# Rests of weights between the table passes, small loads on GpSimd's queue, two output products at attention's end, and TensorE's first expert pass written out

## The chip, the cores and the metric

The kernel runs on 1 core of one Trainium2 chip. The metric is the device time of one launch in microseconds (us): 1806.31 us, the median of 3 runs from 1805.55 to 1809.32. The profiled execution, from which all rows here come, took 1809.38 us, of which the profile covers a span of 1807.4 us from the first to the last instruction.

## The reference, cut to what matters

Two layers over 256 tokens of width 1024. Each layer projects the normalised input once, runs three mixers on columns of that projection, and adds a channel mixer: dense in layer 0, 8 experts of which each token uses 2 in layer 1.

```python
for i in range(DEPTH):                       # 2 layers
    h = rmsnorm(x, norm_mix[i])
    z = h @ w_in[i]                          # [S5 512 | q, k, v 3 x 768 | memory q 512 | gates 3 x 1024]
    y_ssm = ssm_branch(z[..., :c0], ...) @ w_ssm_out[i]   # scan over time, GELU, GLU with w_glu (512 x 1024)
    y_att = dilated_attention(...) @ w_att_out[i]         # QK-norm, rotary with positions
    mem_n = rmsnorm(mem, norm_mem[i])
    y_mem = memory_attention(z[..., c3:c4], mem_n, w_mem_kv[i], ...) @ w_mem_out[i]
    g = sigmoid(z[..., c4:]).reshape(bsz, L, 3, D)
    merged = g[..., 0, :] * y_ssm + g[..., 1, :] * y_att + g[..., 2, :] * y_mem
    x = x + merged @ w_o[i]
    h2 = rmsnorm(x, norm_ffn[i])
    x = x + (swiglu(h2, ...) if i == 0 else moe_swiglu(h2, ...))   # 8 experts, 1024 x 3584
```

## The kernel before, in words

All five engines run programs written out by hand, joined by semaphores. What follows is what the change touches.

**Weights.** A layer's mixer takes its weights in tiles of 128x2048 fp32 (1 MB), numbered in the order of use: 0 to 3 are `w_mem_kv`, 4 to 25 halves of twelve-column-block `w_in`, 26 and 27 `w_glu`, 28 to 30 the last of `w_in` (30 is `IN_FULL`, 256 columns), 31 and 32 `w_ssm_out`, 33 `w_att_out`, 34 and 35 `w_mem_out`, 36 to 39 `w_o`. SP loads a tile into one of three slots of `ring` when TensorE is done with the tile three before. Products are made of two parts: ScalarE's `weights_high` copies the tile to `hi_m` (rounded, two halves of 1024 columns, L1313), and VectorE's `weights_low` subtracts that from the tile to give `ring_lo`, the rest (two halves, L1831). `hi_m` has two buffers, and so ScalarE's copy of tile m waits until TensorE is done with tile m-2:

```python
act.wait_ge(full[n % R], 16 * (n // R + 1))
if i >= 2:
    act.wait_ge(*mixer_use(l, i - 2))
```

TensorE then makes 24 groups of matmuls of each tile: high by high (L694), high by rest (L695) and rest by high (L696). The copy, the rest and the product of one tile stand each at a fixed place of their engine's program, so the order of the three programs decides who waits.

**The start of layer 0.** TensorE does tiles 0 and 1, transposes of `x` (L687), tiles 2 to 6, and then, in the S5 part, tile 7 onward. VectorE does in this order: `setup` (memory's operands and rests of tiles 0 and 1), `constants` (masks' integer grids), `state_rates`, `rotary_angles` (L1898 to L1819), rest of tile 2, `state_coefficients`, rest 3, `input_low` (L1843, the rests of x's transposes), rest 4, `state_matrices` (L1950 on), rest 5, `table_turns`, rest 6, `table_coarse` (L1973, 16 operations), `table_fine` (L1981, 16), `table_folds` (L1988, L1989). The three table functions make the angles for the rotation that turns the complex recurrence into a real scan; ScalarE takes their sines and cosines in two pieces (`tables`, L1354 and L1355).

**The S5 part.** `ssm` starts with rest 7 and then has four rounds v = 0 to 3. A round multiplies TensorE's input part by the tables (L2025, L2026), makes the rest of one tile, adds, scans (L2039), makes another rest and turns the states back (L2045, L2046); GpSimd forms the states from that (L660, L661), and TensorE's `state_output` (L875) waits for GpSimd. On TensorE the four state outputs stand behind the tiles 9, 11, 13 and 15, called here the first to the fourth state output. So round 0 makes rests 8 and 9, round 1 rests 10 and 11, round 2 rests 12 and 13, round 3 rests 14 and 15, and rest 16 follows the rounds. In both orders the first of a round's two rests stands ahead of the scans, the second behind them.

**Small loads.** SP issues, behind tile 2's load and ahead of tile 3's, the six S5 matrices of layer 0 (`load_matrices`, L420 and L423, 128 KB each) and four rows of gains for q and k (L459). GpSimd issues the same six for layer 1 later.

**Attention's end.** Attention runs in 14 slots. In a slot TensorE transposes probabilities (`pr`, L930), multiplies them with the values (L947) and fills in one tile of the list `FILL`. Slot 11 fills in only the transposes of the scan's output (L979), slot 12 tile 30, slot 13 tile 31. After the slots come 12 transposes for the other branches (L687), then tile 32, then tile 33. ScalarE's `soT_hi` (L1546) and VectorE's `soT_lo` are the two parts of the transposed scan output, the operand of tiles 31 and 32.

**Experts.** TensorE's program for the experts (`one_pass`) is a loop of three rounds with two experts each, and the last two experts after it; inside an expert there are shorter loops. ScalarE's is written out, VectorE's has a loop too. The second call of `one_pass` runs only when an expert is over 128 tokens.

Of the kernel before, what the change touches and what calls it, by code (L numbers as in the profile page):

```python
# [16 lines left out]
ALU = mybir.AluOpType  # L17
# [15 lines left out]
def decoder_trunk(nc, x_in, mem_in, positions, norm_mix, w_in, a_re, a_im, log_dt, b_re, b_im,  # L33
# [57 lines left out]
    with ctx:  # L91
# [83 lines left out]
        eb("hole", [P, BANK])  # L175
# [14 lines left out]
        invf = sb1("invf", [P, HD // 2])  # L190
        dist_i = sb1("dist_i", [P, C, SEQ], I32)
        grid_i = sb1("grid_i", [P, 2, SEQ], I32)
        ang = sb1("ang", [P, C, HD // 2])
        turns = sb1("turns", [P, C, HD // 2])
# [233 lines left out]
        def _(sp):  # L428
# [117 lines left out]
        def _(pool):  # L546
# [23 lines left out]
            def second_matrices(l):  # L570
# [27 lines left out]
                nc.gpsimd.memset(mT[:], 0.0).then_inc(sem("mT_zero"), 1)  # L598
                if l == 0:
# [39 lines left out]
            for l in range(L):  # L639
                rsqrt_mean(rs[:, 2:2 + C], ss[:, 2:2 + C], D, (sem("x_squared"), 2 * l + 1), sem("x_rs"))  # L640
                if l == 0:
                    pool.wait_ge(sem("grid_ready"), 1)
                    for c in range(C):
                        for g in range(NG):
                            last = nc.gpsimd.affine_select(out=gmask(c, g), in_=gmask(c, g), compare_op=ALU.is_ge, fill=NEG,
                                                           base=c * P, pattern=[[-1, (c + 1) * P]], channel_multiplier=1)
                    last.then_inc(sem("mask_ready"), 1)
                    second_matrices(0)
                    pool.wait_ge(sem("rope_ready"), 1)
                    pool.wait_ge(params, 16 * 2 * L)  # L650
                    rotary_gains(0)
# [1879 lines left out]
```

## Time and profile before

| | us |
|---|---|
| median of 3 runs | 1806.31 |
| runs | 1805.55, 1806.31, 1809.32 |
| the profiled execution's own time | 1809.38 |
| its span | 1807.4 |
| TensorE busy | 1765.5 (98% of the span) |
| VectorE busy | 1442.2 (80%) |
| ScalarE busy | 1175.7 (65%) |
| GpSimd busy | 112.9 (6%) |
| mean granted TensorE clock | 0.99 of full |

The profiled execution is 3.07 us over the median, so a sum that is made against it is moved by that much to stand on the median. Shares of busy time are means over the whole kernel: the change touches the first 150 us, two stretches of 30 us at 250 and 730 us, and the edges of the expert rounds at 1071, 1318 and 1565 us.

### The profile page before, as it was taken

What the parts mean: (1) busy time and instruction counts of PE and PEld (TensorE: products, weight loads), DVE (VectorE), ACT (ScalarE), POOL (GpSimd) and SP (SyncE); (2) the same over time, 40 slices, a digit from 0 to 9 for tenths busy, and PEclk for the clock granted to TensorE, in tenths of its full rate; (3) what the DMA queues carried; (4) which work ended last, traced back from release to release, by engine and by line L of the source; (5) the groups of instructions that cost most, each with busy time, mean ns of one, the idle gap of its engine ahead of it and who ended that gap; (6) DMA issues with size and microseconds to landing.
All of it is one profiled execution on the core that took longest, in us unless ns stands there. A gap on an engine that the chain in (4) does not pass through costs nothing.

```text
span 1807.4 us, 23380 instructions
## 1 busy us (share of the span) xinstructions
PE 1765.5 (98%) x8755; PEld 1461.0 (81%) x8755; DVE 1442.2 (80%) x1336; ACT 1175.7 (65%) x1320; POOL 112.9 (6%) x159
## 2 busy tenths in 40 slices
PE   7799999999999999999999999999999999999998
PEld 5688888888888888887888878888878888888886
DVE  7987547667756955568899888898888988988987
ACT  6567555654456665656776767777767767777775
POOL 3331000122001300000000000000000000000000
PEclk9899999999999999999999999999999999999999
DMA  6344435755544443377999999999999999999994
GB/s 208 117 141 140 140 99 179 229 188 185 186 139 146 151 145 119 119 267 287 373 364 335 372 348 356 376 341 362 366 330 375 364 334 372 356 364 378 351 374 183
DMA packets 227630, 477.17 MB, mean 264 GB/s; under 512 B 16012, under 2 KB 40712, under 8 KB 227528
## 3 DMA queue, kind: packets, MB, share of 16 engines
q1 hardware_dynamic: 227144, 474.99, 74.0%
q8 instruction: 67, 1.10, 0.2%
q0 software_dynamic: 288, 0.79, 0.2%
q14 instruction: 35, 0.29, 0.0%
q10 hardware_dynamic: 96, 0.02, 0.0%
HBM read 474.71 MB, written 1.05 MB: 263 GB/s over the span
## 4 chain that ended last, share of the span: by engine, by line
PE 91%; DVE 4%; ACT 2%; issue 1%; SPq 1%; DMA 1%; DVEq 0%; ACTq 0%
PE ps L694 28%; PE ps L696 27%; PE ps L695 27%; PE ps L1179 1%; PE ps L947 1%; DVE lo L2231 1%; PE ps L919 1%; PE ps L687 1%; PE ps L1157 1%; PE ps L875 1%; DVE ring_lo L1831 1%; PE ps L930 1%; DMA ring<-in_w_mem_kv 1%; SPq L420 0%; DVE sintab L1981 0%
## 5 line engine op out<-in xcount | busy, mean ns | idle before, releaser
L2231 DVE TENSOR_TENSOR lo<-ring_e,hi 128x2048 fp32r<-128x2048 f32 x288 | 657.7, 2289 | 86.9 <-ACT hi L1598 84.7
L1598 ACT ACTIVATE hi<-ring_e 128x2048 fp32r<-128x2048 f32 x288 | 552.1, 1917 | 168.5 <-PE ps L696 168.0
L694 PE MATMUL ps<-hi,xe_hi 128*128 128x512 f32 x896 | 356.0, 397 | 4.8 <-issue 4.8
L696 PE MATMUL ps<-hi,xe_lo 128*128 128x512 f32 x896 | 350.0, 391 | 0.0
L695 PE MATMUL ps<-lo,xe_hi 128*128 128x512 f32 x896 | 349.9, 390 | 0.0
L1313 ACT ACTIVATE hi_m<-ring 128x1024 fp32r<-128x1024 f32 x160 | 160.7, 1055 | 152.8 <-PE ps L696 150.3
L1831 DVE TENSOR_TENSOR ring_lo<-ring,hi_m 128x1024 fp32r<-128x1024 f32 x160 | 190.6, 1233 | 35.1 <-ACT hi_m L1313 34.6
L696 PE MATMUL ps<-hi_m,xT_lo 128*128 128x512 f32 (+1 forms) x528 | 204.7, 388 | 0.0
L694 PEld LDWEIGHTS ps<-hi,xe_hi 128*128 128x128 f32 x896 | 168.5, 188 | 41.7 <-issue 6.6
L696 PEld LDWEIGHTS ps<-hi,xe_lo 128*128 128x128 f32 x896 | 168.7, 188 | 36.5
L695 PEld LDWEIGHTS ps<-lo,xe_hi 128*128 128x128 f32 x896 | 168.9, 189 | 33.2
L694 PE MATMUL ps<-hi,aT_hi 128*128 128x512 f32 x464 | 181.6, 391 | 0.0
L696 PE MATMUL ps<-hi,aT_lo 128*128 128x512 f32 x464 | 180.8, 390 | 0.0
L695 PE MATMUL ps<-lo,aT_hi 128*128 128x512 f32 x464 | 180.6, 389 | 0.0
L694 PE MATMUL ps<-hi_m,in_hi 128*128 128x512 f32 (+1 forms) x416 | 166.6, 401 | 9.8 <-DVE ring_lo L1831 9.5
L695 PE MATMUL ps<-ring_lo,in_hi 128*128 128x512 f32 (+1 forms) x416 | 159.8, 384 | 0.0
L2231 DVE TENSOR_TENSOR lo<-hT,hi 128x2048 fp32r<-128x2048 f32 x48 | 109.9, 2289 | 14.8 <-ACT hi L1598 14.4
L696 PEld LDWEIGHTS ps<-hi_m,xT_lo 128*128 128x128 f32 x528 | 100.0, 189 | 22.0
L1598 ACT ACTIVATE hi<-hT 128x2048 fp32r<-128x2048 f32 x48 | 92.0, 1916 | 20.8 <-PE ps L696 20.8
L694 PEld LDWEIGHTS ps<-hi_m,in_hi 128*128 128x128 f32 x416 | 79.7, 192 | 29.6 <-DVE ring_lo L1831 9.7
L696 PEld LDWEIGHTS ps<-hi,aT_lo 128*128 128x128 f32 x464 | 87.1, 188 | 18.4
L694 PEld LDWEIGHTS ps<-hi,aT_hi 128*128 128x128 f32 x464 | 87.1, 188 | 18.2 <-issue 0.4
(397 smaller groups left out, 2502.2 us busy)
## 6 DMA issues: line engine op xcount, KB each, us to landing
ring_e<-in_moe_w_gate SPq DMA_DIRECT2D x104, 1024.0 KB, 6.0
ring_e<-in_moe_w_up SPq DMA_DIRECT2D x96, 1024.0 KB, 6.3
ring_e<-in_moe_w_down SPq DMA_DIRECT2D x88, 1024.0 KB, 5.7
ring<-in_w_in SPq DMA_DIRECT2D x50, 1024.0 KB, 5.1
hT<-in_moe_w_down SPq DMA_DIRECT2D x24, 1024.0 KB, 5.8
hT<-in_moe_w_up SPq DMA_DIRECT2D x16, 1024.0 KB, 5.5
ring<-in_ffn_w_gate SPq DMA_DIRECT2D x22, 512.0 KB, 4.0
ring<-in_ffn_w_up SPq DMA_DIRECT2D x22, 512.0 KB, 5.0
```

The costliest lines, as they stand in the source:

```text
L687: last = nc.tensor.transpose(o, a, ident[0:a.shape[0], 0:a.shape[0]])
L694: nc.tensor.matmul(o, x_hi, w_hi, start=first, stop=False, skip_group_check=True)
L695: nc.tensor.matmul(o, x_hi, w_lo, start=False, stop=False, skip_group_check=True)
L696: return nc.tensor.matmul(o, x_lo, w_hi, start=False, stop=end, skip_group_check=True)
L875: last = nc.tensor.matmul(y, by[:, j, r, :], wv[v % 2][:, 2 * i + h, r, :], start=False, stop=r == 1, skip_group_check=True)
L919: last = nc.tensor.matmul(ps[:, bank, col:col + nk], qkT[o:o + HD, 0, hd // 2, c * P:(c + 1) * P], qkT[o:o + HD, 1, hd // 2, 0:nk], start= ...
L930: nc.tensor.transpose(ps[:, 6 + b // 4, b % 4 * P:(b % 4 + 1) * P], pr[:, u % 2, b * P:(b + 1) * P], ident[:])
L947: last = nc.tensor.matmul(ps[:, 5, o:o + v.shape[1]], pT[:, b * P:(b + 1) * P], v, start=first, stop=end, skip_group_check=True)
L1313: nc.scalar.activation(hi_m[:, m % 2, o], ring[:, n % R, o], ACT.Copy).then_inc(sem("mixer_hi_ready"), 1)
L1598: nc.scalar.activation(hi[:, m % H, :], src, ACT.Copy).then_inc(sem("hi_ready"), 1)
L1831: V.tensor_tensor(ring_lo[:, n % R, o], ring[:, n % R, o], hi_m[:, m % 2, o].bitcast(F32), ALU.subtract).then_inc(sem("mixer_lo_ready"), 1)
L2231: last = V.tensor_tensor(lo[:, m % H, :], src, hi[:, m % H, :].bitcast(F32), ALU.subtract)
```

## The change

In layer 0, the rests of tiles 7 and 8 are made between the table passes; each round of the S5 part then makes the rests of tiles one further on (9 and 10, 11 and 12, 13 and 14, 15 and 16), and none follows the rounds. Layer 1 keeps the old order there. `rotary_angles` moves from ahead of rest 2 to behind rest 6 (its buffers with it), and `constants` from behind `setup` to ahead of it. On ScalarE the squares of memory and of x move behind `state_steps` and behind copy 4, the rotary sines and `tables` behind `mT`, and the copy of tile 8 ahead of them. The ten small loads move from SP's queue to GpSimd's, behind the arrival of x. On GpSimd the causal masks come earlier, and `second_matrices` is cut into `second_input` (ahead of x's mean square) and `second_output` (behind it). In both layers, attention's slot 11 makes the transposes of the scan's output and then tile 30, slots 12 and 13 make tiles 31 and 32, and tile 33 follows the 12 transposes; ScalarE's copies and VectorE's rests shift by a place. In the experts, TensorE's loop over three rounds is written out for the first pass.

```diff
@@ SP
-            load_matrices(nc.sync, 0)
-            for l in range(L):
-                sp.dma_start(gqk[:, l, 0, :], g_q[l:l + 1, :].to_broadcast([P, HD])).then_inc(params, 16)
-                sp.dma_start(gqk[:, l, 1, :], g_k[l:l + 1, :].to_broadcast([P, HD])).then_inc(params, 16)
@@ GpSimd
             ssm_zeros(0)
+            pool.wait_ge(sem("x_loaded"), 16)
+            load_matrices(nc.gpsimd, 0)
+            for l in range(L):
+                for qk, g in enumerate((g_q, g_k)):
+                    pool.dma_start(gqk[:, l, qk, :], g[l:l + 1, :].to_broadcast([P, HD])).then_inc(params, 16)
...
             for l in range(L):
+                if l == 0:
+                    second_input(0)
                 rsqrt_mean(rs[:, 2:2 + C], ss[:, 2:2 + C], D, (sem("x_squared"), 2 * l + 1), sem("x_rs"))
...
+                    second_output(0)
                 for v in range(NV):
+                    if l == 0 and v == 1:
+                        pool.wait_ge(sem("rope_ready"), 1)
+                        pool.wait_ge(params, 16 * 2 * L)
+                        rotary_gains(0)
@@ TensorE, attention's slots and the experts
-        FILL += [("glu", 0), ("glu", 1), (IN_FULL - 1, 0), (IN_FULL - 1, 1), ("transposes", 0)]
+        FILL += [("glu", 0), ("glu", 1), (IN_FULL - 1, 0), (IN_FULL - 1, 1), (IN_FULL, 0)]
         AHEAD = len(FILL)
-        FILL += [(IN_FULL, 0), ("out", 0)]
+        FILL += [("out", 0), ("out", 1)]
...
                         elif t == IN_FULL:
+                            transpose_scan_output()
                             part(n_in + LAST_IN + 2, 0, 1, inputs_split, KD, 256)
...
-                part(n + 1, 0, 1, soT, KS)
...
-                    with pe.Fori(0, NE // 2 - 1) as p:
-                        expert(p + pair0, 0, False)
-                        expert(p + pair0, 1, False)
+                    if pair0 == 0:
+                        for p in range(NE // 2 - 1):
+                            expert(p, 0, False)
+                            expert(p, 1, False)
@@ ScalarE
-                    if s < AHEAD - 1:
+                    if s < AHEAD:
                         weights_high(l)
...
-                weights_high(l)
                 act.wait_ge(sem("columns_used"), COL_TILES * l + FIRST_OUT)
                 branch_gate(0, "ssm_gate_ready")
+                branch_gate(1, "attention_gate_ready")
+                weights_high(l)
+                branch_gate(2, "memory_gate_ready")
@@ VectorE
                 state_rates(l)
-                rotary_angles()
                 weights_low(l)
...
                 table_turns()
                 weights_low(l)
+                rotary_angles()
                 table_coarse(l)
+                weights_low(l)
                 table_fine()
+                weights_low(l)
                 table_folds()
 
             def ssm(l):
 
-                weights_low(l)
+                if l > 0:
+                    weights_low(l)
...
-            setup()
             constants()
+            setup()
```

VectorE's rows from the coarse pass to the first rest of round 0, in layer 0, before (L1831 is a rest, here tiles 7 and 8; L1973, L1981 and L1988 with L1989 are the coarse pass, the fine pass and the folds; L2025 opens the S5 part's round 0):

```order
L1973 SCALAR_TENSOR_TENSOR sintab<-ramp,spT,costab 128x128 x16
L1975 TENSOR_TENSOR spT<-spT 128x16
L1977 MEMSET stat 128x1
L1981 SCALAR_TENSOR_TENSOR sintab<-ramp,spT,sintab 128x128 x16
L1988 TENSOR_SCALAR sintab<-sintab 128x512
L1989 SCALAR_TENSOR_TENSOR costab<-sintab 128x512
L1988 TENSOR_SCALAR sintab<-sintab 128x1536
L1989 SCALAR_TENSOR_TENSOR costab<-sintab 128x1536
L1831 TENSOR_TENSOR ring_lo<-ring,hi_m 128x1024 x2
L2025 TENSOR_TENSOR z<-ps,costab 128x1024
L2026 TENSOR_TENSOR z<-ps,sintab 128x1024
L1831 TENSOR_TENSOR ring_lo<-ring,hi_m 128x1024 x2
```

The same place of the changed kernel (L1844 is a rest, here tiles 7 and 8; L1986, L1994 and L2001 with L2002 are the passes and the folds):

```order
L1986 SCALAR_TENSOR_TENSOR sintab<-ramp,spT,costab 128x128 x16
L1988 TENSOR_TENSOR spT<-spT 128x16
L1990 MEMSET stat 128x1
L1844 TENSOR_TENSOR ring_lo<-ring,hi_m 128x1024 x2
L1994 SCALAR_TENSOR_TENSOR sintab<-ramp,spT,sintab 128x128 x16
L1844 TENSOR_TENSOR ring_lo<-ring,hi_m 128x1024 x2
L2001 TENSOR_SCALAR sintab<-sintab 128x512
L2002 SCALAR_TENSOR_TENSOR costab<-sintab 128x512
L2001 TENSOR_SCALAR sintab<-sintab 128x1536
L2002 SCALAR_TENSOR_TENSOR costab<-sintab 128x1536
L2040 TENSOR_TENSOR z<-ps,costab 128x1024
L2041 TENSOR_TENSOR z<-ps,sintab 128x1024
```

Both rests now stand ahead of L2040, which was L2025; one of them stood behind it.

ScalarE's rows at attention's end before, from slot 10's columns on (L1514 copies transposed probabilities, L1526 makes probabilities, L1321 takes columns into `z`, L1313 is the copy of tile 32, L1546 is `soT_hi`):

```order
L1321 ACTIVATE z<-ps,rs 128x512 x2
L1514 ACTIVATE pT<-ps 128x512
L1526 ACTIVATE pr,rm<-ps,rm,scale_mq 128x256 x2
L1546 ACTIVATE soT_hi<-ps 128x1024
L1514 ACTIVATE pT<-ps 128x512
L1321 ACTIVATE z<-ps,rs 128x256 x2
L1313 ACTIVATE hi_m<-ring 128x1024 x2
```

The same place of the changed kernel (L1328 is the copy of tile 32, L1562 is `soT_hi`, L1336 takes columns):

```order
L1336 ACTIVATE z<-ps,rs 128x512 x2
L1530 ACTIVATE pT<-ps 128x512
L1542 ACTIVATE pr,rm<-ps,rm,scale_mq 128x256 x2
L1328 ACTIVATE hi_m<-ring 128x1024 x2
L1562 ACTIVATE soT_hi<-ps 128x1024
L1336 ACTIVATE z<-ps,rs 128x256 x2
L1530 ACTIVATE pT<-ps 128x512
```

The copy of tile 32 stood behind `soT_hi`; it stands ahead of it now, and by the rule of the two `hi_m` buffers it waits for TensorE's end of tile 30.

## Rows read from the trace of the kernel before

In a timeline a row has its start and its duration in us, and in brackets the idle time ahead of it with what ended it.

**Rows 1.** the page: the chain that ended last, shares of the span by engine

```profile
PE 91%; DVE 4%; ACT 2%; issue 1%; SPq 1%; DMA 1%; DVEq 0%; ACTq 0%
```

**Rows 2.** TensorE's waits: line, what it waited for, us, times, longest us

```profile
PE ps L694 <- DVE ring_lo L1831: 11.0, 2, 9.5
PE ps L687 <- DVE xT_lo L1843: 4.5, 1, 4.5
```

**Rows 3.** the chain, 0 to 160 us: start us, us, what

```profile
8.33 8.47 SPq L420
21.63 10.40 DMA ring<-in_w_mem_kv
```

**Rows 4.** the page: loads of a weight tile, KB each, median us to landing

```profile
ring<-in_w_in SPq DMA_DIRECT2D x50, 1024.0 KB, 5.1
```

**Rows 5.** windows: us, busy by engine, granted clock (PEclk), DMA share, GB/s

```profile
69.90:83.50 13.60, 5.93 (x15) 4.68 (x16) 12.94 (x20) 7.16 (x10) 1.16 (x4) 0.52 0.00 0
738.00:742.00 4.00, 4.00 (x22) 4.00 (x22) 2.41 (x4) 1.30 (x2) 0.00 (x0) 0.57 0.00 0
1071.00:1075.00 4.00, 2.38 (x11) 1.64 (x10) 4.00 (x6) 1.03 (x1) 0.00 (x0) 1.00 0.96 364
1321.50:1325.00 3.50, 3.50 (x11) 2.74 (x10) 2.03 (x1) 0.03 (x1) 0.00 (x0) 0.56 0.83 266
```

**Rows 6.** VectorE's timeline, layer 0's tables and round 0

```profile
21.92 0.17 DVE L1898 CAST pos<-pos_i 128x2 f32<-128x2 int32 x1
24.87 2.35 DVE L1831 TENSOR_TENSOR ring_lo<-ring,hi_m 128x1024 fp32r<-128x1024 f32 x2
42.23 0.43 DVE L1950 TENSOR_TENSOR z<-z,spT 128x256 f32<-128x256 f32 x1
57.91 4.28 DVE L1973 SCALAR_TENSOR_TENSOR sintab<-ramp,spT,costab 128x128 f32<-128x128 f32 x16
64.04 8.48 DVE L1981 SCALAR_TENSOR_TENSOR sintab<-ramp,spT,sintab 128x128 f32<-128x128 f32 x16
78.57 1.22 DVE L2025 TENSOR_TENSOR z<-ps,costab 128x1024 f32<-128x1024 f32 x1
87.62 2.33 DVE L1831 TENSOR_TENSOR ring_lo<-ring,hi_m 128x1024 fp32r<-128x1024 f32 x2
```

**Rows 7.** ScalarE's timeline, 30 to 80 us

```profile
32.05 2.00 ACT L1313 ACTIVATE hi_m<-ring 128x1024 fp32r<-128x1024 f32 x2 [2.50 <-DMA ring<-in_w_mem_kv]
77.80 1.56 ACT L1355 ACTIVATE costab<-costab,half_pi 128x1536 f32<-128x1536 f32 x1
```

**Rows 8.** GpSimd's timeline: states of round 0, a small load

```profile
93.53 1.31 POOL L661 TENSOR_TENSOR z<-z 128x512 f32<-128x512 f32 x1
...
332.10 1.36 POOL L420 DMA_DIRECT2D b_raw_next<-in_ssm_b_re  x1
```

**Rows 9.** TensorE's timeline: tile 0's end, three state outputs

```profile
18.46 0.39 PE L696 MATMUL ps<-hi_m,mem_lo 128*128 128x512 f32 x1
...
99.40 1.94 PE L875 MATMUL ps<-z,cT 128*32 128x128 f32 x32
...
114.70 1.94 PE L875 MATMUL ps<-z,cT 128*32 128x128 f32 x32
...
143.49 1.94 PE L875 MATMUL ps<-z,cT 128*32 128x128 f32 x32
```

**Rows 10.** TensorE's timeline at attention's end, layer 0

```profile
260.00 0.73 PE L930 MATMUL ps<-ident,pr 128*128 128x128 f32 x4 [1.92 <-ACT pr L1526]
262.08 0.56 PE L694 MATMUL ps<-hi_m,in_hi 128*128 128x256 f32 x1
269.46 0.48 PE L694 MATMUL ps<-hi_m,soT_hi 128*128 128x512 f32 x1
...
282.39 0.48 PE L694 MATMUL ps<-hi_m,xT_hi 128*128 128x512 f32 x1 [0.22 <-issue]
```

**Rows 11.** TensorE's waits in the experts, 820 to 1807 us

```profile
PE ps L694 <- issue: 4.8, 4, 2.0
```

More of the change, by code:

```diff
@@ L174, in decoder_trunk @@
         mT = eb("mT", [P, NJ // 4, P])
-        eb("hole", [P, BANK])
+        invf = eb("invf", [P, HD // 2])
+        ang = eb("ang", [P, C, HD // 2])
+        turns = eb("turns", [P, C, HD // 2])
+        eb("hole", [P, BANK - (2 * C + 1) * HD // 2])
         costab = eb("costab", [P, NJ, HALF])
@@ L568, in rotary_gains, with second_input @@
                 last.then_inc(sem("rgain_ready"), 1)
-            def second_matrices(l):
+            def second_input(l):
                 if l == 0:
@@ L629, in _ @@
                                               base=SPAN - c * P, pattern=[[1, (c + 1) * P]], channel_multiplier=-1))
-            ssm_zeros(0)
+            pool.wait_ge(sem("grid_ready"), 1)
+            for c in range(C):
+                for g in range(NG):
+                    last = nc.gpsimd.affine_select(out=gmask(c, g), in_=gmask(c, g), compare_op=ALU.is_ge, fill=NEG,
+                                                   base=c * P, pattern=[[-1, (c + 1) * P]], channel_multiplier=1)
+            last.then_inc(sem("mask_ready"), 1)
+            ssm_zeros(0)
+            pool.wait_ge(sem("x_loaded"), 16)
[3 more added lines that the diff above has]
+                    pool.dma_start(gqk[:, l, qk, :], g[l:l + 1, :].to_broadcast([P, HD])).then_inc(params, 16)
             def rsqrt_mean(dst, src, count, of, done, eps=EPS):
@@ L668, in _ @@
                     ssm_zeros(1)
-                    second_matrices(1)
+                    second_input(1)
+                    second_output(1)
                     rotary_gains(1)
@@ L949, in weigh_values, with transpose_scan_output @@
                     return last
+                def transpose_scan_output():
+                    pe.wait_ge(sem("glu_done"), l + 1)
+                    pe.wait_ge(sem("columns_used"), acc[0] - 1)
+                    pair = 2 * (acc[0] % 2)
+                    for q in range(KS):
+                        for c in range(C):
+                            col = (q % 2 * C + c) * P
+                            last = nc.tensor.transpose(ps[:, pair + q // 2, col:col + P],
+                                                       sout[:, c, q * P:(q + 1) * P], ident[:])
+                    acc[0] += 1
+                    last.then_inc(sem("columns_done"), 1)
                 for s in range(UNITS + 2):
@@ L970, in mixer @@
                             part(n_in + GLU_TILE + i, 0, 1, gTs, KS)
[L971 to L982 removed]
                         elif t == "out":
[L984 to L985 removed]
+                            if i == 0:
+                                pe.wait_ge(sem("columns_used"), COL_TILES * l + SOUT_COL)
+                            part(n_in + OUT_TILE + i, 0, 1, soT, KS)
                         elif t == IN_FULL:
+                            transpose_scan_output()
                             part(n_in + LAST_IN + 2, 0, 1, inputs_split, KD, 256)
@@ L1542, in mixer @@
                             cols[0] += 1
-                        elif t == "transposes":
+                        elif t == IN_FULL:
                             act.wait_ge(sem("columns_done"), cols[0] + 1)
@@ L2158, in attention @@
                         V.memset(stat[:, 0, 3:4], 0.0).then_inc(sem("glu_done"), 1)
-                    if s >= 1 and FILL[s - 1][0] == "transposes":
+                    if FILL[s][0] == IN_FULL:
                         dve.wait_ge(sem("soT_hi_ready"), l + 1)
@@ L2493, in experts @@
                     V.memset(rstat[:, 0:1], 0.0).then_inc(sem("x_final"), 1)
+            constants()
             setup()
-            constants()
             for l in range(L):
```

77 lines of the change are left out of this document (26 added, 51 removed).

## Prediction

> **What bounds the kernel now.** I read first the chain of waits by engine: TensorE holds 91% of it [rows 1], so the change can give back only time in which TensorE stands idle, and time in which it runs at half clock. The table of TensorE's waits says where that is: 11.0 us for rests of weight tiles, 9.5 of them in one piece, and 4.5 us for the rests of x's transposes [rows 2]; in the experts 4.8 us in four pieces that wait for nothing the profile shows [rows 11]. The chain in order of time names the cause of the 4.5 us: SP stood 8.47 us in the issue of one small matrix, and then tile 3's load took 10.40 us from 21.63 [rows 3] where a tile's load takes 5.1 [rows 4]. The copy of tile 3 waited for it [rows 7]. The windows give the second price of a wait: after the 9.5 us TensorE ran its 5.93 busy us up to 83.5 at a granted 0.52, the lower of its levels (1.2 GHz), which costs 5.93 x 0.48 = 2.9 us; after a wait of 1.9 us the granted clock is 0.57 for 4 us (1.7 us lost), after a 2.0 us wait 0.56 for 3.5 us (1.5 us), and around 1071, where TensorE is busy 2.38 us of 4.00, it stays at 1.00 [rows 5].
>
> **The start of layer 0.** Tile 3's slot is free when TensorE is done with tile 0, at 18.46 + 0.39 = 18.9 [rows 9]. With no small loads ahead of it on SP, its load lands between 18.9 + 5.1 = 24.0 and 18.9 + 10.4 = 29.3 [rows 3, 4]. The small matrices still move in that time, now from GpSimd's queue, so I take 27.0, 5.0 us earlier than before, and let copy 3, rest 3, the operand's rests, rest 4 and `state_matrices` (42.23 before [rows 6]) all come 5.0 earlier. The 4.5 us wait goes. Ahead of round 0 VectorE now has two things more: the rotary angles, 24.87 - 21.92 = 2.95 us, and rest 8, 2.35 us [rows 6]. So round 0 opens at 78.57 - 5.0 + 2.95 + 2.35 = 78.9: the 5 us are spent on VectorE. The sines of the second piece used to end 79.36 - 76.2 = 3.15 us behind the folds [rows 6, 7]; now they end at 82.05, and copy 9 stands behind them, its first half 1.0 us [rows 7]: rest 9 starts at 83.05. Rest 8 started at 79.36 + 1.1 for `mT` + 1.0 = 81.45. The states of round 0, ready at 93.53 + 1.31 = 94.84 before [rows 8], are 1.6 us later, at 96.4. TensorE took them at 99.40, since it was still at tile 9 [rows 9]. It has done tiles 7 to 9 earlier now (rest 9 is done at 85.4, tile 9 at 91.1), so it waits there for 5.3 us and goes on 3.0 us earlier than before. The long wait is moved, from ahead of tile 7 to ahead of the first state output, and it is shorter.
>
> What follows costs that again. After 5.3 us idle I expect the lower clock, 2.9 us. Between the first two state outputs lie 114.70 - 99.40 = 15.30 us, of them 1.94 for the output, some 2 for inputs, and two tiles of 5.7 [rows 9]. Each round's second rest is now one tile further on, and its copy waits for TensorE's end of a tile that comes only after the last state output: rest 12 for tile 10, rest 14 for tile 12, rest 16 for tile 14. From there to the states it is 1.0 for the half copy and 94.84 - 87.62 = 7.2 for rest, turns and GpSimd [rows 6, 8]. Tile 10 ends at 96.4 + 7.6 + 2.9 = 106.9, the second states are ready at 115.1, and TensorE's own 96.4 + 15.3 + 2.9 = 114.6 waits 0.5. In the same way the third output comes at 131.0. In the last round TensorE has no inputs to make between its tiles: it gets there at 144.0, tile 14 ends at 138.6, the states are ready at 146.8. That is 3.3 us over 143.49 [rows 9], and 2.8 us of wait bring the lower clock once more, 1.7 us by the row after 1.9 us. The start: +5.0 us. Bounds: without the clock drops (2.9 + 1.7) it is near 0; with the load at 24.0 it is 3.0 less at the first output, of which tile ends and second rests give 1 to 2 back in the last; with the load at 29.3 it is 2.3 more.
>
> At nothing I cost: `constants` (2.2 us ahead of rest 0, under VectorE's idle start), the squares and sines (ScalarE has gaps of 2.5 us and more there [rows 7]), and GpSimd's causal masks. The ten issues cost GpSimd up to 1.36 us each [rows 8], at most 14 us from x's landing; if ScalarE's memory columns came late by this, the lower end is nothing and the upper end about 1 us of copy 4.
>
> **Attention's end, in each layer.** Removed: the 1.92 us wait for `pr` [rows 10] with its 1.7 us of lower clock [rows 5], for tile 30 now covers the probabilities. TensorE starts tile 30 at 260.00 - 1.92 = 258.1; from 262.08 to 269.46 it took 7.4 us for tile 30 and 0.8 of values, about 1 of it lost to the clock, so the tile alone ends near 264.0, and 1.3 us of attention follow. But the copy of tile 32 now stands ahead of `soT_hi` on ScalarE, and waits for tile 30's end: 264.0 + 2.0 for the copy + 1.0 for `soT_hi`, half of such a pair [rows 7], + 1.2 for `soT_lo` (the price of 1024 columns, 1.22 [rows 6]) = 268.4 with handing over. TensorE waits there for 3.1 us; by [rows 5] that costs 1.7 us of clock. From tile 31's start to tile 33's it took 282.39 - 269.46 = 12.93 us [rows 10]: 268.4 + 12.93 + 1.7 = 283.0. The parts of `oT` are no longer hidden by tile 32: 0.5 us (estimate: 1.2 for two operations of 512 columns, less the transposes behind the first four), and tile 34's rest comes 0.4 later. So +1.5 us in each layer, +3.0 in both; without the clock drop -0.4.
>
> **The experts.** Removed: the waits at the edges of rounds, 4.8 us [rows 11], and 1.5 us of lower clock after 1318 [rows 5]: -6.3. The four pieces lie where the loop goes back, around 1071 and 1318; at 1565, where the last pair follows in straight code, there is none. The bounds are -6.3 and, if the longer code brings waits of its own of the same size, 0; I take -6.3, since the straight code behind 1565 has none.
>
> **Sum.** +5.0 + 3.0 - 6.3 = +1.7 us on the profile's 1809.38, which is 1811.1; the profiled execution was 3.07 over the median, so 1808.0 on the median. A measurement of this kernel can tell about 0.2%, 3.6 us, from no change: I forecast no change that can be told.
>
> **A rule that speaks against the moved loads.** The coarse and fine passes have 16 operations of one shape each, 4.28 and 8.48 us [rows 6]; GpSimd was at work beside the fine one. The Trainium skill, page "SBUF — State Buffer", section "SBUF: two separate sides", says that VectorE and GpSimd exclude each other on a shared port pair, and that loads issued from GpSimd's queue starve while VectorE holds it. By the first the 4.2 us only move to another operation, and the sum stands at 1808.0. By the second the small matrices come late; no row shows a load starved.
>
> As a mechanism of this kernel: if each of the ten issues stood behind half a rest (1.2 us [rows 6]) besides its own 1.36, they would end 12 us later, near 40, where `state_matrices` is due at 37.2; GpSimd's `second_input` and with it the share of `state_matrices` that waits for the input matrices would be up to 3 us late: 1811.0. This is one half of rival C.
>
> **The rivals.**
> A, the sum above: 1808.0, its own range 1805.5 to 1811. Chance 0.39.
> B, faster: TensorE's clock stays up after the new waits, as around 1071 [rows 5], or they are shorter than I make them. The sum has 2.9 + 1.7 at the start and 1.7 in each attention, 8.0 us in all: 1800.0. A fine pass that GpSimd no longer doubles would give the first states up to 4.2 us earlier, of which the later rounds take most again; it decides from 2 us of earliness, for then TensorE hardly waits at the first output. For it: the waits are moved to places where I know them only. Against it: three of the four rows after waits of 1.9 us and more show the drop. 0.31.
> C, slower: VectorE reaches round 0 later. Tile 3's load lands no earlier than 29.3, because GpSimd's loads still share the 16 engines with it, or GpSimd, behind its ten issues, is late with the input matrices. Each us on VectorE there is a us at the first state output: +2.3 by the load and up to 4.2 if GpSimd's matrices now fall beside `state_matrices` and rest 7 as well as the fine pass: 1810.3 to 1814.5. It decides from 2 us. 0.24.
> D, the change does not do what it says in the experts: the longer straight code is fetched late somewhere, and the 6.3 us come back: 1814.3. 0.06.
>
> **How the numbers follow.** The likeliest is A, 1808.0. B's end with half of the lock's 4.2 us on top of 1800.0, less what the rounds take, is about 1799; C's and D's are up to 1816. That leaves out no more than 2 in 10. Faster than 1802.7 is nearly all of B, 0.30; slower than 1809.9 is C and D nearly whole and a part of A, 0.31; the rest, 0.39, is the same.
>
> **What the changed profile would show.** Right: tile 3's load issued near 19 and landed by 27; no wait for x's rests; a wait of 4 to 6 us for GpSimd's states at the first state output near 96, and 2 to 3 us at the fourth near 147; each with a granted clock near 0.5 behind it; a wait of some 3 us for `soT_lo` ahead of tile 31 in both layers; no wait for `pr`; no "issue" wait over 0.4 us in the experts. Wrong: the tile load as late as before; TensorE's wait for tile 7 still over 5 us; a clock at 1.00 behind the waits (B); new waits inside the expert rounds (D); or a wait at a place that I have not named, above all between 147 and 170, where VectorE no longer has rest 16 to make and I count that as no gain.

## The result, and the profile after

The changed kernel takes 1810.31 us (median of 20 runs, from 1809.73), the kernel before 1808.07 us (median of 20, from 1805.55 to 1811.97). The ratio is 1.0015, 95% interval 1.0008 to 1.0021: 2.7 us slower (1.4 to 3.8), under the 0.2% that the forecast had called the bound of what can be told. One run of the 20 took 3576.21 us; it is left out of the ratio, and nothing here explains it.

The profiled execution took 1809.95 us, its span is 1807.9 us. The page's busy times and the chain by engine:

```profile
PE 1762.8 (98%) x8755; PEld 1458.3 (81%) x8755; DVE 1444.3 (80%) x1336; ACT 1175.5 (65%) x1320; POOL 122.3 (7%) x169
...
PE 89%; ACT 2%; DVE 1%; issue 0%; POOL 0%; ACTq 0%; DVEq 0%
```

TensorE is still 98% busy and still the chain, as in [rows 1]. Its waits (line, what it waited for, us in total, times, longest) show what took the place of [rows 2]:

```profile
PE ps L883 <- POOL z L668: 10.7, 4, 6.0
PE ps L702 <- DVE ring_lo L1844: 6.8, 3, 4.6
PE ps L702 <- DVE soT_lo L2178: 6.1, 2, 3.0
...
PE ps L702 <- DVE xT_lo L1869: 1.1, 2, 0.5
PE ps L695 <- POOL z L589: 1.0, 1, 1.0
PE ps L702 <- issue: 0.7, 1, 0.7
PE ps L695 <- DVE xT_lo L1856: 0.5, 1, 0.5
```

The 4.5 us for x's rests are down to 0.5 us (L1856), and the rests of weight tiles have fallen from 11.0 to 6.8. In their place stand 10.7 us for GpSimd's states, four times, and 6.1 us for the low part of the scan output, twice, and 1.0 us for GpSimd's share of the input matrices (L589). The wait without a cause is 0.7 us, where [rows 11] had 4.8. What the change removed is about as long as what it added: all rows of the list together are 36.0 us before and 38.5 us after. The single places, in TensorE's timeline of the start (three of the four state outputs) and of attention's end in layer 0:

```profile
94.45 1.92 PE L883 MATMUL ps<-z,cT 128*32 128x128 f32 x16 [5.97 <-POOL z L668]
...
112.56 1.94 PE L883 MATMUL ps<-z,cT 128*32 128x128 f32 x32 [0.75 <-POOL z L668]
...
145.51 2.76 PE L883 MATMUL ps<-z,cT 128*32 128x128 f32 x32 [3.66 <-POOL z L668]
```

```profile
260.21 1.04 PE L967 MATMUL ps<-ident,z 128*128 128x128 f32 x8
261.49 0.39 PE L702 MATMUL ps<-hi_m,in_hi 128*128 128x256 f32 x1 [0.24 <-ACT z L1336]
...
271.85 0.47 PE L702 MATMUL ps<-hi_m,soT_hi 128*128 128x512 f32 x1 [3.04 <-DVE soT_lo L2178]
```

The first state output starts 4.95 us earlier than in [rows 9], the second 2.1 earlier, the fourth 2.0 later. At attention's end the probabilities cost no wait now, but tile 31 starts at 271.85 after 3.04 us idle. The granted clock (the number ahead of the last two) behind these waits, and around the first edge of the expert rounds:

```profile
95.00:102.00 7.00, 7.00 (x46) 5.91 (x43) 6.06 (x12) 0.00 (x0) 4.87 (x8) 0.74 0.01 4
145.00:151.00 6.00, 5.49 (x41) 4.48 (x42) 5.93 (x6) 0.10 (x1) 0.46 (x1) 0.72 0.22 84
271.80:275.80 4.00, 3.96 (x11) 3.16 (x12) 2.71 (x4) 3.97 (x5) 0.00 (x0) 0.62 0.01 2
751.90:755.90 4.00, 3.98 (x17) 3.27 (x18) 2.69 (x3) 3.97 (x5) 0.00 (x0) 1.00 0.01 2
1071.00:1085.00 14.00, 14.00 (x64) 11.51 (x64) 14.00 (x10) 10.15 (x7) 0.00 (x0) 1.00 0.92 320
```

Behind the 6.0 us wait it is 0.74 over 7 us (1.8 us lost), behind the 3.7 us wait 0.72 over 6 us (1.7 lost), behind the wait at tile 31 0.62 over 4 us in layer 0 (1.5 lost) and 1.00 in layer 1, where the wait is the same 3.04 us. Around 1071 TensorE is busy throughout; in [rows 5] it was for 2.38 us of 4.

VectorE, GpSimd and ScalarE at the start of layer 0, the rows that answer to [rows 6 to 8]:

```profile
36.43 0.44 DVE L1963 TENSOR_TENSOR z<-z,spT 128x256 f32<-128x256 f32 x1
...
53.95 1.88 DVE L1830 SCALAR_TENSOR_TENSOR ang<-turns,ang 128x64 f32<-128x64 f32 x1
55.86 1.80 DVE L1831 TENSOR_SCALAR ang<-ang 128x64 f32<-128x64 f32 x1
...
57.84 6.34 DVE L1986 SCALAR_TENSOR_TENSOR sintab<-ramp,spT,costab 128x128 f32<-128x128 f32 x16
...
66.61 4.28 DVE L1994 SCALAR_TENSOR_TENSOR sintab<-ramp,spT,sintab 128x128 f32<-128x128 f32 x16
...
76.93 1.22 DVE L2040 TENSOR_TENSOR z<-ps,costab 128x1024 f32<-128x1024 f32 x1
...
80.98 2.36 DVE L1844 TENSOR_TENSOR ring_lo<-ring,hi_m 128x1024 fp32r<-128x1024 f32 x2 [1.70 <-ACT hi_m L1328]
```

```profile
53.84 1.91 POOL L604 TENSOR_TENSOR cT<-cT,spT 128x1024 f32<-128x1024 f32 x1 [7.60 <-ACT cT L1303]
55.70 1.91 POOL L605 TENSOR_TENSOR gT<-cT,spT 128x1024 f32<-128x1024 f32 x1
...
93.04 1.27 POOL L668 TENSOR_TENSOR z<-z 128x512 f32<-128x512 f32 x1
```

```profile
25.39 2.01 ACT L1328 ACTIVATE hi_m<-ring 128x1024 fp32r<-128x1024 f32 x2 [1.76 <-DMA ring<-in_w_mem_kv]
```

The second rest of the second round (tile 12) and the ScalarE copy that it waits for, which itself waits for TensorE's end of tile 10:

```profile
104.19 2.01 ACT L1328 ACTIVATE hi_m<-ring 128x1024 fp32r<-128x1024 f32 x2 [9.90 <-PE ps L704]
```

```profile
105.28 2.36 DVE L1844 TENSOR_TENSOR ring_lo<-ring,hi_m 128x1024 fp32r<-128x1024 f32 x2 [4.18 <-ACT hi_m L1328]
```

Tile 3's load is there at 25.4 (32.0 in [rows 7]); `state_matrices` starts 5.8 us earlier, round 0 only 1.6 us earlier (76.93 against 78.57), and the first rest of round 0 waits for ScalarE until 80.98. Two of the small angle operations take 1.8 us, where the others of their kind take 0.2, and the coarse pass takes 6.34 instead of 4.28, all beside GpSimd's L604 to L607; the fine pass, alone now, is down from 8.48 to 4.28. The time that the two engines cost each other has moved. The Trainium skill, page "SBUF — State Buffer", section "SBUF: two separate sides", says that GpSimd and, in certain of its operations, VectorE share a port pair, and that the one that starts first holds it for a whole instruction. The trace agrees: the small operation L1830 took 1.88 us beside GpSimd's L604 of 1.91 us.

### The profile page after: what moved, and what is told of

The parts are those of the page before. It is cut to its first block, busy times and chain, and to the rows that moved or that the text cites. A ratio compares the mean times of both kernels' runs of the same rounds, so it can differ in the third digit from the quotient of the medians.

```text
span 1807.9 us, 23235 instructions
## 1 busy us (share of the span) xinstructions
PE 1762.8 (98%) x8755; PEld 1458.3 (81%) x8755; DVE 1444.3 (80%) x1336; ACT 1175.5 (65%) x1320; POOL 122.3 (7%) x169
## 4 chain that ended last, share of the span: by engine, by line
PE 89%; ACT 2%; DVE 1%; issue 0%; POOL 0%; ACTq 0%; DVEq 0%
PE ps L702 27%; PE ps L704 27%; PE ps L703 26%; PE ps L1189 1%; PE ps L927 1%; PE ps L955 1%; PE ps L1167 1%; PE ps L695 1%; PE ps L883 1%; PE ps L938 1%; ACT hi_m L1328 0%; PE ps L1262 0%; PE ps L1263 0%; PE ps L918 0%; ACT z L1336 0%
## 5 line engine op out<-in xcount | busy, mean ns | idle before, releaser
L1328 ACT ACTIVATE hi_m<-ring 128x1024 fp32r<-128x1024 f32 x160 | 160.8, 1056 | 166.0 <-PE ps L704 164.2
L1844 DVE TENSOR_TENSOR ring_lo<-ring,hi_m 128x1024 fp32r<-128x1024 f32 x160 | 190.4, 1231 | 40.9 <-ACT hi_m L1328 40.1
L2246 DVE TENSOR_TENSOR lo<-hT,hi 128x2048 fp32r<-128x2048 f32 x48 | 109.8, 2288 | 14.1 <-ACT hi L1611 13.6
L703 PEld LDWEIGHTS ps<-lo,aT_hi 128*128 128x128 f32 x464 | 87.1, 188 | 17.9
```

Source lines behind the costliest of these rows:

```text
L703: nc.tensor.matmul(o, x_hi, w_lo, start=False, stop=False, skip_group_check=True)
L1328: nc.scalar.activation(hi_m[:, m % 2, o], ring[:, n % R, o], ACT.Copy).then_inc(sem("mixer_hi_ready"), 1)
L1844: V.tensor_tensor(ring_lo[:, n % R, o], ring[:, n % R, o], hi_m[:, m % 2, o].bitcast(F32), ALU.subtract).then_inc(sem("mixer_lo_ready"), 1)
L2246: last = V.tensor_tensor(lo[:, m % H, :], src, hi[:, m % H, :].bitcast(F32), ALU.subtract)
```

## The experiments

Each kernel was timed against the kernel before on the same chip (e1 to e4, e10 and e11 on one, e5 to e8 on a second, e9 and e12 on a third), so kernels of different chips are compared by their ratios. Differences in us are the ratio's distance from 1 times 1808. The theory: the three parts of the change add up, each by what the trace shows in its own stage, and in the start what costs is the place of the rests. The rivals stand in the expectations.

| run | what it is | median us | ratio to before (95%) |
|---|---|---|---|
| e1 | experts alone | 1800.33 | 0.9957 (0.9943 to 0.9970) |
| e2 | attention's end alone | 1814.32 | 1.0029 (1.0019 to 1.0039) |
| e3 | start alone | 1814.51 | 1.0033 (1.0021 to 1.0045) |
| e4 | start, rest 8 put back | 1803.97 | 0.9969 (0.9957 to 0.9982) |
| e5 | attention's end, `soT_hi` first | 1804.63 | 0.9986 (0.9976 to 0.9995) |
| e6 | start, rest 8 early, rounds as before | 1802.34 | 0.9973 (0.9963 to 0.9984) |
| e7 | e4 with the small loads on SP | 1808.67 | 1.0001 (0.9992 to 1.0010) |
| e8 | all, mended as in e4 and e5 | 1793.08 | 0.9920 (0.9906 to 0.9933) |
| e9 | e8 with attention's end as before | 1794.48 | 0.9923 (0.9909 to 0.9937) |
| e10 | all, mended as in e5 and e6 | 1792.44 | 0.9909 (0.9894 to 0.9924) |
| e11 | e10 with the angles behind round 0 | 1792.24 | 0.9911 (0.9898 to 0.9925) |
| e12 | e8 with attention's end as changed | 1802.29 | 0.9963 (0.9949 to 0.9976) |

### The three parts alone

e1 is the last hunk for TensorE in the diff above, alone:

> Only TensorE's first expert pass written out. Theory (the parts add up, each by its own stage): the waits at the edges of rounds and the lower clock behind one of them go, so -6.3 to -6.7 us against the kernel before, a ratio of 0.9963 to 0.9965. Rival (the changed kernel's loss is in the experts: the longer code costs somewhere else, or moves the two writes at the end): no more than -3 us, a ratio of 0.998 or over.

Measured: 7.8 us faster (5.4 to 10.3), profiled span 1797.8. Between 1000 and 1800 us TensorE waits once, and not without a cause:

```profile
PE ps L1252 <- DVE y_lo L2458: 0.2, 1, 0.2
```

The timelines give a sharper number than the runs: from TensorE's first expert matmul to its last it is 972.9 to 973.0 us in each of the seven profiles with the pass written out, and 979.5 to 981.6 us in each of the seven with the loop (979.68 before). So the edit is worth 6.5 to 8.6 us in this stage, and what varies is the loop. Ahead of the first expert matmul some profiles have one more wait without a cause: 0.9 us here, 0.7 in the changed kernel, 0.3 before; it is no price of the straight code, for e4, which has the loop, shows 1.5 us there and e9, which has not, none. The page "Runtime: NRT & Kernel Launch" of the Trainium skill, section "Instruction fetch mechanics", says that a taken branch to code outside the fetched window stalls until it is fetched. The trace agrees with it: in the seven profiles with the loop TensorE is idle for 1.6 to 2.4 us at each jump back, at 7 of the 14 jumps for another 0.8 to 2.2 us some 5 to 7 us later, and not where the loop is left. The profile itself names no cause of these waits.

e2 holds the hunks of `FILL`, of the slots and of the merge:

> Only attention's end, in both layers. Theory: a wait of 3.0 us for the low part of the scan output takes the place of the 1.9 us wait for the probabilities, with the lower clock behind it in some places and not in others: +0.4 to +1.9 us a layer, together +2.3 us (up to +3.6 where the clock drops in both), a ratio of 1.0013 to 1.002. Rival (the attention edit is a gain, and the start alone loses): -2 to 0 us, 0.999 to 1.000.

Measured: 5.2 us slower (3.4 to 7.1). The theory's direction holds; its +2.3 lies under the interval, and its upper end of 3.6 is passed by the measured value. Why is taken up with e12.

e3 holds all other hunks:

> Only the start of layer 0: rests, angles, squares, masks and small loads. Theory: TensorE is 5 us early at the first state output and 2 us late at the fourth, +3.2 us at attention's end: a ratio of about 1.0018. The wait of 6 us ahead of the first state output and that of 4 us ahead of the fourth are there, with lower clocks behind them. Rival (the 3 us are an accident of one profile): within 1 us of before, 1.000.

Measured: 6.0 us slower (3.8 to 8.1). The rival falls: the loss is no accident of one profile. The theory's +3.2 was too small; this kernel's own profile is 5.5 us late at attention's end. The waits are where they were in the changed kernel (5.96 us at the first state output at 95.31, the fourth at 147.03), and from there to attention's end it takes 2.0 us longer than before, behind the wait at a granted 0.57 over 6 us. Its experts' loop has no part in the 6.0 us: it takes 979.46 us, 979.68 before.

The parts alone sum to -7.8 + 5.2 + 6.0 = +3.4 us; together they give +2.7 (1.4 to 3.8). They add up within the intervals.

### The start: which rest costs

e4 undoes one thing in e3, the place of rest 8 and with it that of all later rests of the rounds:

```diff
                 table_fine()
-                weights_low(l)
                 table_folds()
@@ def ssm, behind the four rounds
-                if l > 0:
-                    weights_low(l)
+                weights_low(l)
```

> The start's edits, but with one rest only between the table passes: rest 7 stays between the coarse and the fine pass, rest 8 goes back behind the products of round 0, and every round makes the rests that it made before. Theory (each round's second rest is one tile too far on, and rest 8 delays round 0): TensorE has no wait over 1.5 us at the first and at the fourth state output; the fourth comes near 137 to 139 us instead of 145.5, and the whole is -4 to -7 us against before, a ratio of 0.996 to 0.998. Rival (the loss of the start comes from GpSimd's small loads and from angles and tables that GpSimd slows, wherever the rests stand): the fourth state output comes no earlier than 143 us, ratio 1.000 or over.

Measured: 5.6 us faster than before (3.3 to 7.8), so 11.6 us better than e3 by this one edit. TensorE's timeline at the first two state outputs, and its windows:

```profile
93.90 1.94 PE L883 MATMUL ps<-z,cT 128*32 128x128 f32 x32
...
109.20 1.94 PE L883 MATMUL ps<-z,cT 128*32 128x128 f32 x32
```

```profile
80.00:100.00 20.00, 20.00 (x131) 16.41 (x131) 19.86 (x31) 11.61 (x48) 8.13 (x10) 0.95 0.33 106
100.00:120.00 20.00, 20.00 (x156) 16.30 (x155) 16.70 (x23) 14.08 (x66) 6.91 (x6) 1.00 0.42 132
120.00:140.00 20.00, 20.00 (x137) 16.41 (x136) 18.25 (x24) 11.16 (x32) 12.01 (x4) 1.00 0.44 136
```

No wait stands ahead of an output, the rounds are TensorE's own time (20.00 of 20 us busy), and the fourth output starts at 138.0. The rival, that the small loads or GpSimd's slowing of the angles and tables carry the loss, falls: both are still there (the slowed operations now cost VectorE 5.4 us, 5.3 in the changed kernel).

e6 keeps rest 8 early and takes only the shift out of the rounds:

```diff
                     last.then_inc(sem("bu_used"), 1)
-                    weights_low(l)
+                    if l > 0 or v > 0:
+                        weights_low(l)
```

> Only the start's edits, with rest 8 between the fine pass and the folds as in the change, but no rest in its old place in round 0: round 0 makes rest 9 alone, and the later rounds and the rest 16 behind them stand as before. Theory (what costs is that each round's second rest waits for a tile that TensorE makes after the last state output, not where rest 8 stands): tile 8 starts without the wait of 4.5 us, a wait of some 4 us for rest 9 comes instead, no wait at the first and fourth state output, the fourth at 136 to 138 us: a ratio of 0.996 to 0.997, up to 2 us better than with rest 8 put back. Rival (rest 8 ahead of round 0 costs as such): the fourth state output near 145 us again, ratio over 1.001.

Measured: 4.9 us faster (2.9 to 6.7), the fourth output at 136.34 in its profile, after a wait of 2.9 us for rest 9 and none at the outputs. By the ratio it is not better than e4. Rest 8 ahead of round 0 costs nothing as such. What cost in the change is the shift by a tile: the second rest of each round waited for a tile that TensorE makes only behind the last state output.

e7 is e4 with the four lines of the small loads on SP again:

> The start's edits with one rest between the table passes (as in the run with rest 8 put back), but the ten small loads back on SP's queue. Theory (the small loads ahead of tile 3's load are what makes TensorE wait 4.5 us for x's rests): the wait of 4 to 5 us near 32 us is back, everything on VectorE up to round 0 is 4 to 5 us later, and the kernel is 3 to 5 us slower than with them on GpSimd, a ratio of 0.998 to 1.001 against before. Rival (the load of tile 3 was late for the traffic, whichever queue issues it, or the rounds swallow it): within 1.5 us of the run with the loads on GpSimd, 0.996 to 0.998.

Measured: no change against before (0.9992 to 1.0010), so 5.8 us slower than e4. TensorE's waits from 20 to 100 us:

```profile
PE ps L701 <- DVE ring_lo L1839: 8.6, 2, 5.0
PE ps L694 <- DVE xT_lo L1851: 6.1, 1, 6.1
```

The wait for x's rests is back, 6.1 us. The move to GpSimd's queue is worth what the forecast gave it ahead of round 0, and without it the other edits of the start gain nothing; whether it would gain as much without them was not run. GpSimd's ten issues in the changed kernel took 0.54 to 1.36 us each and landed in 4.1 to 6.4 us, so no starved load shows here. One price of the move was not foreseen: from the end of TensorE's last product to the end of the span it is 5.5 to 5.6 us in the five profiles with the small loads on SP and 6.0 to 6.6 us in the nine with them on GpSimd. Why stays open.

### Attention's end

e5 changes the order on ScalarE in e2, and nothing else:

```diff
-                    if s < AHEAD:
+                    if s < AHEAD - 1:
                         weights_high(l)
...
                             nc.scalar.activation(flat(soT_hi), flat_banks(pair, 2), ACT.Copy).then_inc(
                                 sem("soT_hi_ready"), 1)
+                            weights_high(l)
```

> Only attention's end, as in the change, but with ScalarE's high part of the scan output ahead of the copy of tile 32. Theory (the wait of 3.0 us for the scan output's low part exists only because the copy of tile 32 waits for TensorE's end of tile 30): that wait goes, tile 31 starts some 3.3 us earlier than with the attention edit as it was, and the kernel is -4 to -6 us against before, a ratio of 0.997 to 0.998. Rival (two output products in a row wait anyway, for the copy of tile 32 or for the other branches' operands): about as the attention edit alone, 1.000 to 1.003.

Measured: 2.5 us faster than before (0.9 to 4.3), and 7.8 us better than e2. ScalarE's timeline there:

```profile
259.36 1.02 ACT L1548 ACTIVATE soT_hi<-ps 128x1024 fp32r<-128x1024 f32 x1
263.97 2.00 ACT L1315 ACTIVATE hi_m<-ring 128x1024 fp32r<-128x1024 f32 x2 [3.59 <-PE ps L696]
```

The high part is made at 259.36, under tile 30, and the copy of tile 32 waits behind it, where nobody waits for it. The cause of the 3.0 us wait is shown. The gain is smaller than I expected, though, and e2's loss is larger. e9 and e12 put the other two forms of attention's end into the mended whole e8:

> The mended whole (rest 8 put back, experts written out), but with attention's end as in the kernel before. It prices the attention edit where nothing else differs. Theory (mended attention is worth what its trace showed, 2.5 to 2.9 us a layer): +5 us against the mended whole, a ratio of 0.9945 to 0.995. Rival (it is worth what the run with it alone showed, 2.5 us in both layers): 0.9930 to 0.9935.

> The mended whole, but with attention's end as the change has it, the copy of tile 32 ahead of the scan output's high part. Theory (this place alone costs a wait of 3.0 us in each layer, and the lower clock behind it now and then): +6 to +9 us against the mended whole, a ratio of 0.9955 to 0.997. Rival (the wait is partly made up for by the operands of the other branches, which come late anyway): +3 us, 0.9935.

Measured: e9 0.9923 (0.9909 to 0.9937) against e8's 0.9920, which is no difference that can be told; e12 0.9963, on the same chip as e9 and 7.2 us over it by the ratio (7.8 by the medians). So the form of the change costs some 7 us against the form before, and the mended form gains little over the form before. In e9 the theory falls; the rival's 2.5 us fit the interval, though the value lies below its range. In e12 the theory held. The timelines show most of the reason. The stage from the scan output's transposes to tile 31, and from there to tile 33, in us, without and with the lower clock behind the wait:

| form | to tile 31 | to tile 33 | layers with lower clock |
|---|---|---|---|
| before (1.92 us wait) | 10.9, or 12.4 | 12.9 | 5 of 14 |
| changed (3.04 us wait) | 11.6 | 14.1, or 15.6 | 3 of 6 |
| mended (no wait) | 8.35 | 14.1 | 0 of 8 |

In the kernel before, both layers of the profiled execution have the lower clock, and in e9's neither has, behind the same wait (windows of 4 us there):

```profile
256.00:260.00 4.00, 3.95 (x34) 3.98 (x35) 2.71 (x4) 1.46 (x2) 0.00 (x0) 1.00 0.00 0
732.00:736.00 4.00, 3.56 (x31) 3.59 (x32) 3.10 (x5) 1.86 (x4) 0.00 (x0) 1.00 0.00 0
```

So a layer's form before costs 23.8 us and, in 5 of 14 cases, 1.5 more; the change's 25.7, and in 3 of 6 cases 1.5 more. That is 1.9 + 0.2 = 2.1 us a layer, 4.3 in both, within e2's interval. The mended form costs 22.5 us a layer with no lower clock, 1.3 under the form before and 0.5 more for its clock: 3.7 us in both, within e5's interval.

e12's difference from e9 is more than 4.3. In the two profiles it is 7.4 us: 3.5 and 2.0 in the two attention stages (the lower clock fell in one layer of e12 and in none of e9), 1.3 already at the fourth state output, and 0.6 elsewhere. The start's edits are the same in e8, e9 and e12, and yet they have their fourth state output at 137.8, 139.6 and 140.9. Tile 7 starts at 65.7, 66.7 and 67.6 us there, so 0.9 and 1.8 us of it are older than round 0. They come from tile 0, whose first matmuls run at the lower level in e9 (9 of them) and e12 (14) and at the full one in e8; the first two rows are e12's, the third is e8's:

```profile
12.24 0.63 PE L703 MATMUL ps<-ring_lo,xT_hi 128*128 128x512 f32 x1
...
17.36 0.62 PE L703 MATMUL ps<-ring_lo,xT_hi 128*128 128x512 f32 x1
```

```profile
12.00 0.39 PE L703 MATMUL ps<-ring_lo,xT_hi 128*128 128x512 f32 x1
```

Start to start it is 0.43 us for one of them against 0.23. The remaining 0.8 and 1.2 us come behind tile 8, where the granted clock between 80 and 95 us is 0.94, 0.86 and 0.80. Whether e12's other executions began like this one stays open, and with it how much of the 7.8 us between the medians belongs to attention.

### The mended whole

> The whole change with its two places mended: one rest between the table passes with rest 8 back in round 0, and the high part of the scan output ahead of the copy of tile 32. Theory (the parts add): -5.6 from the start and -7.8 from the experts as measured alone, -4 to -6 from attention: -17 to -20 us, a ratio of 0.989 to 0.991. Rival (gains of the parts share waits and don't add): no better than -12 us, 0.9935.

> The whole change mended at two places, but with rest 8 between the fine pass and the folds and no first rest in round 0, instead of rest 8 put back. Theory (the state outputs are limited by tile ends, not by where rest 8 stands): the fourth state output near 136.3 us as in the start alone, 1.5 us earlier than with rest 8 put back: a ratio of 0.991 to 0.992. Rival (the 1.6 us seen between the two starts alone are the lower clock falling differently): the same as with rest 8 put back, 0.992 to 0.993.

> The same, with the rotary angles moved out of VectorE's chain ahead of round 0, to behind round 0's products (their sines behind copy 10, GpSimd's gains ahead of the third states). Theory (up to the first state output VectorE is the bound, and beside GpSimd's products the angles cost 5.7 us instead of 3): the first states are 3 to 5 us earlier, TensorE's wait for rest 7 falls from 5 us to 1 to 2 us, the later rounds take 0 to 1 us of it: -2 to -4 us against the run before, a ratio of 0.989 to 0.991. Rival (GpSimd's products then stand beside the coarse pass and slow that by as much, and the angles fill round 1's only pause): no gain, 0.991 to 0.993.

Measured: e8 is 14.5 us faster than before (12.1 to 17.0), less than the sum of e1, e4 and e5 as I had set it (17 to 20) and about their sum as measured (7.8 + 5.6 + 2.5 = 15.9). e10 (16.5 us faster than before) cannot be told from e8: its fourth output is at 137.88, e8's at 137.84, and not near 136.3. So the theory falls, although the ratio is as low as it said, and the rival holds: e6's profile had a granted clock of 0.91 from 80 to 100 us and e10's has 0.83, which is 1.6 us. In e11 the first states come earlier, as the theory had it (the first output at 89.82 against 93.79), but VectorE and GpSimd in its profile show what takes the place:

```profile
52.18 4.29 DVE L1988 SCALAR_TENSOR_TENSOR sintab<-ramp,spT,costab 128x128 f32<-128x128 f32 x16
...
58.30 5.09 DVE L1846 TENSOR_TENSOR ring_lo<-ring,hi_m 128x1024 fp32r<-128x1024 f32 x2
63.32 5.31 DVE L1996 SCALAR_TENSOR_TENSOR sintab<-ramp,spT,sintab 128x128 f32<-128x128 f32 x16
```

```profile
53.90 4.33 POOL L604 TENSOR_TENSOR cT<-cT,spT 128x1024 f32<-128x1024 f32 x1 [7.61 <-ACT cT L1303]
...
60.17 2.15 POOL L606 TENSOR_TENSOR cT<-cT,gT 128x512 f32<-128x512 f32 x1
62.27 2.27 POOL L607 TENSOR_TENSOR cT<-cT,gT 128x512 f32<-128x512 f32 x1
```

GpSimd's products now stand beside rest 7 (5.09 us for 2.36) and the fine pass (5.31 for 4.28), and not beside the coarse pass as the rival had it; with them GpSimd's own products take up to 2.3 times their 1.9 and 1.3 us. TensorE waits for rests in six pieces, 8.9 us from 40 to 300. Of the 4.0 us at the first output 2.0 are left at the fourth (135.89 against 137.88) and 0.6 at the end of the profile, and the medians of e11 and e10 are 0.2 us apart: no gain, as the rival said, though by another way.

## Why the prediction was right

**The sum.** Forecast was +1.7 us, measured +2.7 (1.4 to 3.8), and the range held the time. The parts were less near than their sum: alone they measure +6.0, +5.2 and -7.8 where +5.0, +3.0 and -6.3 were forecast, so two losses and a gain were all set too small, and in the sum the errors partly cancel. That is luck; the waits and their places are not. Of the 2.3 us between 1808.0 and 1810.31, 1.8 are the base: the three runs known then had their median at 1806.31, twenty have it at 1808.07.

**The start, +5.0.** The places held one by one, most of them a little early: tile 3's load landed at 25.4 (27.0 forecast), `state_matrices` at 36.4 (37.2), round 0 at 76.9 (78.9), the first rest at 81.0 (83.05), the states at 94.3 (96.4), the wait for them 6.0 (5.3), the fourth output at 145.5 (146.8) after a wait of 3.7 (2.8). Inside VectorE's chain two errors cancel: the rotary angles took 5.7 us, not 2.95, and the coarse pass 6.3, not 4.3, because GpSimd's products fell on them, while the fine pass fell from 8.5 to 4.3. At attention's end the profile is 3.2 us late; alone, the part measures +6.0 (3.8 to 8.1). e4 and e6 show that the step "each round's second rest is now one tile further on" carries the loss. The lower clock behind the first output cost 1.8 us, not 2.9.

**Attention's end, +3.0.** The mechanism was right to the tenth: 3.1 us of wait forecast, 3.04 in both layers; e5 shows its cause. The size was too small, +5.2 (3.4 to 7.1) alone. Both terms for the lower clock were booked in full in each layer. As a thing removed ("the 1.92 us wait for `pr` with its 1.7 us of lower clock") it is there in 5 of 14 layers at 1.5 us, 0.5 on the mean; as a thing added it is there in 3 of 6, 0.8 on the mean. The two errors nearly cancel, and so they don't explain the size. What is left is plain time: without any lower clock the stage is 1.9 us longer in each layer, where the forecast, with both clock terms out, has about 1.3 (1.5 less 1.7, plus the 1.5 that the profile before holds). Half of these 0.6 us lie ahead of tile 31, half between it and tile 33 (14.1 us where 12.93 and 0.9 for late operands were forecast). That makes +4.3 for both layers; the other 0.9 us up to the measured 5.2 are within the interval.

**The experts, -6.3.** 6.7 us by the timelines, 7.8 (5.4 to 10.3) alone. The rival that the straight code waits elsewhere fell: the 0.7 us without a cause ahead of the first expert matmul are there in kernels with the loop too.

**The small loads.** e7 prices the move at 5.8 us by itself; I had it as 5.0 us ahead of round 0 and nothing left of it, which was right because the angles and rest 8 spent it.

**The rivals.** B needed the clock to stay up behind the new waits; of the four that its sum names it did so at one, in layer 1's attention. C needed the tile load or GpSimd's input matrices late. The load was early and VectorE's `state_matrices` too; TensorE did wait 1.0 us for GpSimd's share (L589, at 44.4 us), which GpSimd began at 33.2, not behind its loads but behind ScalarE's copy of the coefficients.

## What to carry to other kernels

Where an engine's program is an order written by hand, moving one weight preparation a place forward moves every later one in the loop as well; ask of each which product it waits for, and whether that product stands behind a wait for the same engine. A change that sums to nearly nothing may hold a gain and a loss of 8 and 11 us, and its trace, read by stages, tells which edit to undo: two reorderings of a line or two took this one from a ratio of 1.0015 to 0.9920. And a clock drop behind a short wait, read from one profile, is a chance and not a term: count over several executions or layers how often it follows the same wait, for the one that goes as for the one that comes.

## What the runs showed of the hardware that I had not expected

The granted clock falls or stays behind waits of the same length: behind 1.92 us in 5 of 14 layers, behind 3.04 us in 3 of 6, each time worth 1.5 us. Over all TensorE waits past 25 us in the fourteen profiles it was low in the 4 us behind 12 of 35 of 1.5 to 2.5 us, 6 of 9 of 2.6 to 3.1 us, and all 37 of 3.5 to 9.9 us. So the long waits of the start could be booked with it, and those at attention's end could not.

At the start of the kernel the same holds without a wait that differs: in 6 of the 14 profiles the first 6 to 14 matmul rows of tile 0 run at the lower level (0.63 us where 0.39 is usual), and up to 1.8 us of that reach round 0. The windows give 1.00 for the granted clock there all the same; the durations of the matmuls tell it.

The loop's two jumps back, with the lower clock that sometimes follows, cost TensorE 6.5 to 8.6 us, more in one kernel than in another with the same loop, while the same code written out takes 972.9 to 973.0 us in seven kernels.

An operation of VectorE on 64 columns took 1.8 us instead of 0.2 beside a GpSimd product, and a rest of 2.36 us took 5.09. Moving the work only chose which operation paid: ahead of round 0 VectorE lost 5.3 us by it in the changed kernel and 5.5 us in e11.
